# A state scan whose halves are exchanged on VectorE, and queries formed already turned, in a fused S5 + MLA + MoE layer

## The reference, cut to what matters

```python
bu_r = jnp.einsum('lbgp,gnp->lbgn', ul, bbr)
bu_i = jnp.einsum('lbgp,gnp->lbgn', ul, bbi)
_, _, h_r, h_i = lax.associative_scan(_ssm_combine, (a_r, a_i, bu_r, bu_i), reverse=(d == 1), axis=0)
y = y + einsum('lbgn,gpn->lbgp', h_r, c_re[d]) - einsum('lbgn,gpn->lbgp', h_i, c_im[d])
...
q = (_rms_norm(c_q, q_norm_g) @ w_uq).reshape(bsz, seq, N_HEADS, 64 + 32)
q_rope = _rope(q[..., 64:], cos, sin)          # [t1*cos - t2*sin, t1*sin + t2*cos]
s = (einsum('bqhd,bkhd->bhqk', qn, k_nope) + einsum('bqhr,bkr->bhqk', qr, k_rope)) * scale
p = softmax(s);  o = einsum('bhqk,bkhd->bqhd', p, v)
```

## Time and profile before

| what | value |
|---|---|
| time, median of 3 runs (lowest to highest) | 1645.67 us (1643.55 to 1646.66) |
| the profiled execution: its time, its span | 1644.44 us, 1642.6 us |
| PE, DVE, ACT, POOL busy over the span | 93 %, 49 %, 25 %, 26 % |
| one head (scores of step 0 to scores of step 0 of the next, fourth head) | 326.87 to 383.73 us, 56.86 us |

### The profile page before, as it was taken

The page is one execution under the profiler, slowest core; times in us unless marked ns, Lnnn a source line. Parts: engine busy times, 40 slices in busy tenths (PEclk is TensorE's granted clock), DMA queues, the critical chain, the costliest instruction groups (busy, mean ns, idle before and its releaser), DMA issues. The chain is left out here.

```text
span 1642.6 us, 18705 instructions
## 1 busy us (share of the span) xinstructions
PE 1524.1 (93%) x5878; PEld 857.1 (52%) x5878; DVE 797.0 (49%) x1578; ACT 407.0 (25%) x712; POOL 432.8 (26%) x444
## 2 busy tenths in 40 slices
PE   7996999999999979999989999999999999999980
PEld 4545778777777754555534444444444444444430
DVE  1485766777666742488824333333333333333325
ACT  1313554555555441122100001001101001101105
POOL 0000000000000000023423455555555555555520
PEclk9998999999999989999999999999999999999995
DMA  9005000000021018010546999999999999999956
GB/s 256 20 26 68 14 15 14 10 13 10 10 90 25 16 48 310 40 39 27 219 161 230 368 367 367 375 358 360 376 366 354 370 360 360 368 366 359 338 138 218
DMA packets 107457, 321.51 MB, mean 196 GB/s; under 512 B 39638, under 2 KB 56686, under 8 KB 82450
## 3 DMA queue, kind: packets, MB, share of 16 engines
q1 hardware_dynamic: 84002, 261.47, 42.7%
q0 software_dynamic: 23408, 59.45, 15.0%
HBM read 275.93 MB, written 51.72 MB: 199 GB/s over the span
## 5 line engine op out<-in xcount | busy, mean ns | idle before, releaser
L1777 DVE STREAM_TRANSPOSE moe_xgT<-moe_xg 128x1024 f32<-128x1024 f32 x65 | 132.0, 2031 | 421.3 <-DMA moe_xg<-x_d,moe_idx 421.3
L1592 POOL DMA_INDIRECT moe_xg<-x_d,moe_idx x260 | 263.5, 1013 | 116.1 <-issue 60.6
L1172 POOL DMA_INDIRECT slot_d<-all_entry,all_dest_i x48 | 48.0, 1000 | 770.4 <-DVE all_dest_i L1418 758.2
L1666 PE MATMUL moe_p_y<-mixers_ring_b,moe_hT 128*128 128x512 f32 x520 | 233.9, 592 | 0.9 <-DVE moe_hT L1788 0.9
L1646 PE MATMUL moe_p_gu<-mixers_ring_b,moe_xgT 128*128 128x512 f32 x512 | 225.0, 592 | 0.0
L1714 ACT ACTIVATE moe_sig<-moe_p_gu 128x256 f32<-128x256 f32 x65 | 25.0, 384 | 586.6 <-PE moe_p_gu L1646 586.6
L1603 POOL DMA_INDIRECT sum_d<-moe_y,moe_idx x65 | 105.4, 1622 | 244.8 <-DMA sum_d<-moe_y,moe_idx 208.0
L1666 PEld LDWEIGHTS moe_p_y<-mixers_ring_b,moe_hT 128*128 128x128 f32 x520 | 98.7, 190 | 125.0 <-issue 123.9
L1646 PEld LDWEIGHTS moe_p_gu<-mixers_ring_b,moe_xgT 128*128 128x128 f32 x512 | 95.1, 191 | 107.1 <-issue 107.1
L762 PE MATMUL att_p_o<-att_v,att_prT 128*128 128x64 f32 x1024 | 125.5, 276 | 9.5 <-ACT att_prT L852 9.5
L762 PEld LDWEIGHTS att_p_o<-att_v,att_prT 128*128 128x128 f32 x1024 | 119.3, 192 | 26.0 <-ACT att_prT L852 26.0
(11 more groups left out here) (329 smaller groups left out, 1936.0 us busy)
## 6 DMA issues: line engine op xcount, KB each, us to landing
mixers_ring_b<-in_we_down_dram SPq DMA_DIRECT2D x65, 1024.0 KB, 10.1
mixers_ring_b<-in_we_gate_dram SPq DMA_DIRECT2D x32, 1024.0 KB, 10.3
mixers_ring_b<-in_we_up_dram SPq DMA_DIRECT2D x32, 1024.0 KB, 17.5
mixers_ring_a<-in_we_gate_dram SPq DMA_DIRECT2D x17, 1024.0 KB, 10.0
mixers_ring_a<-in_we_up_dram SPq DMA_DIRECT2D x17, 1024.0 KB, 16.9
mixers_o<-in_we_gate_dram SPq DMA_DIRECT2D x16, 1024.0 KB, 10.1
mixers_o<-in_we_up_dram SPq DMA_DIRECT2D x16, 1024.0 KB, 17.2
all_x_sb<-in_x_dram SPq DMA_DIRECT2D x16, 512.0 KB, 9.6
```

The costliest lines, as they stand in the source:

```text
L1172: nc.gpsimd.indirect_dma_start(k.slot_d[:, :], bass.IndirectOffsetOnAxis(ap=k.dest[:, n:n + 1], axis=0), k.entry[:, t, q, :], None).then_i ...
L1592: nc.gpsimd.indirect_dma_start(xg[:, u, g, :], None, x1_quarters, bass.IndirectOffsetOnAxis(ap=idx[:, c, g:g + 1], axis=0), bounds_check=N ...
L1666: last = nc.tensor.matmul(p_y[:, half * 512:(half + 1) * 512], hT[:, u, kk, :], k.moe_dn[v][:, kk * D + half * 512:kk * D + (half + 1) * 512],
L1777: nc.vector.transpose(xgT[:, u].rearrange("p k (g i) -> p g k i", g=NQ), xg[:, u].rearrange("p g (j k) -> p g k j", k=KD)).then_inc(x_turn ...
```

## The change

Four things change.

1. The scan's halves are now exchanged on DVE. `effects` makes one product per group instead of two (4 instead of 8 in each of its calls), into its own half of `p_v` for each direction. `states` gets the swapped product by two instructions on 64 partitions each, which read one half and write the other (`crossed`), both before and after the scan, and adds the two scaled copies into one `gc`. `outputs` then has 3 products per group instead of 5 (12 instead of 20), and `ed2`, `gsn` and `other_edge` are gone.
2. The queries come out of PE already turned: 2 parts of 2 products with 512 moving columns each take the place of 2 parts of 8 products with 96 columns, and the parts "qT" (2 parts of 4 transposes) are gone. There are 5 parts in a head instead of 7, so "v" moves from step 6 to step 4.
3. The query weights hold the 32 rotary columns twice, the second time with halves swapped, so that the 128 rows of a product hold all that the rotation needs. DVE multiplies the 64 rotary rows by a table of cosines and signed sines (`keep_rope`, one instruction of 64 x 512 per part); `rotate` (6 instructions of 128 x 128) is gone. The keys' rotary rows are stored twice, so the score product contracts over 128 rows instead of 96. ACT copies only the 64 rows without rotation, raises the new semaphore `q_nope`, and DVE raises `part_kept` for the query parts.
4. The loading of a head's weights takes 4 DMAs instead of 2, and one more DMA brings the table.

The core of the diff:

```diff
 def load_heads(eng, k, h, u):
-    eng.dma_start(k.wq[:, u], k.w_uq[0].rearrange("(k p) n -> p k n", p=P)[:, :, bass.ds(h * DQ, DQ)]).then_inc(k.head_in[u], 16)
+    eng.dma_start(k.wq[:, u, :, 0:DQ], wq[:, :, bass.ds(h * DQ, DQ)]).then_inc(k.head_in[u], 16)
+    eng.dma_start(k.wq[:, u, :, DQ:DQ + 16], wq[:, :, bass.ds(h * DQ + (NOPE + 16), 16)]).then_inc(k.head_in[u], 16)
+    eng.dma_start(k.wq[:, u, :, DQ + 16:P], wq[:, :, bass.ds(h * DQ + NOPE, 16)]).then_inc(k.head_in[u], 16)
...
-        PARTS = ("q", "q", "k", "k", "qT", "qT", "v")
+        PARTS = ("q", "q", "k", "k", "v")
...
                 if what == "q":
-                    for r in range(4):
-                        t = second * 4 + r
-                        for kk in range(2):
-                            last = nc.tensor.matmul(p_p[:, r * DQ:(r + 1) * DQ], k.cqT[:, kk, t * P:(t + 1) * P],
-                                                    wq[:, u, kk, :], start=(kk == 0), stop=(kk == 1))
+                    for kk in range(2):
+                        last = nc.tensor.matmul(p_p[:, :], wq[:, u, kk, :], k.cqT[:, kk, second * 512:(second + 1) * 512],
+                                                start=(kk == 0), stop=(kk == 1))
...
             def effects(b, d):
-                for part in range(2):
-                    for r in range(GB):
-                        last = nc.tensor.matmul(p_v[:, part, r, :], vsT[:, d * GB + r, part * N:part * N + P],
-                                                U[:, bass.ds(b * GB + r, 1), :].rearrange("p a n -> p (a n)"), start=True, stop=True)
+                for r in range(GB):
+                    last = nc.tensor.matmul(p_v[:, d, r, :], vsT[:, d * GB + r, :],
+                                            U[:, bass.ds(b * GB + r, 1), :].rearrange("p a n -> p (a n)"), start=True, stop=True)
...
-                        nc.tensor.matmul(out, ed1[:, gd, 1 - d:1 - d + T, :].rearrange("p j c -> p (j c)"), gc[:, gd, d:d + NC],
-                                         start=False, stop=False)
-                        last = nc.tensor.matmul(out, ed2[:, gd].rearrange("p j c -> p (j c)"), gsn[:, gd, d:d + NC],
+                        last = nc.tensor.matmul(out, ed1[:, gd, 1 - d:1 - d + T, :].rearrange("p j c -> p (j c)"), gc[:, gd, d:d + NC],
                                                 start=False, stop=(d == 1))
...
+            def keep_rope(h, u, second, p_p=p_p):
+
+                cols = slice(second * 512, (second + 1) * 512)
+                dve.wait_ge(q_nope, h * 2 + second + 1)
+                nc.vector.scalar_tensor_tensor(qT[NOPE:P, u, cols], p_p[NOPE:P, :], SCALE, k.rope[NOPE:P, cols],
+                                               ALU.mult, ALU.mult).then_inc(part_kept, 1)
...
+            def crossed(ch, src, sin_t):
+
+                nc.vector.tensor_tensor(rb[0:N], src[N:P], sin_t[N:P], ALU.mult)
+                ch.link(nc.vector.tensor_tensor(rb[N:P], src[0:N], sin_t[0:N], ALU.mult))
...
-                tt(ra, p_v[:, 0], cos_t[:, own_rows, :], ALU.mult)
-                ch.link(tt(rb, p_v[:, 1], sin_t[:, own_rows, :], ALU.mult))
+                tt(ra, p_v[:, d], cos_t[:, own_rows, :], ALU.mult)
+                crossed(ch, p_v[:, d], sin_t[:, own_rows, :])
                 dve.sem_inc(v_read, 1)
-                ch.link(tt(ra, ra, rb, ALU.add))
+                ch.link(tt(ra, ra, rb, ALU.subtract))
...
-                tt(gc[:, own_rows, off:off + NC], gr[:, :, :], cos_t[:, own_rows, :], ALU.mult)
-                tt(gsn[:, own_rows, off:off + NC], gr[:, :, :], sin_t[:, own_rows, :], ALU.mult).then_inc(g_done, 1)
+                tt(ra, gr[:, :, :], cos_t[:, own_rows, :], ALU.mult)
+                crossed(ch, gr, sin_t[:, own_rows, :])
+                tt(gc[:, own_rows, off:off + NC], ra, rb, ALU.add).then_inc(g_done, 1)
...
                     if t == 0:
                         states(chs, h, u, 0)
                     if t == 1:
                         add_kernels(h)
-                        other_edge(chs, h, 0)
                     if t == 2:
                         states(chs, h, u, 1)
-                    if following and t == ROTATE:
-                        rotate(ch, h + 1)
+                    if following and t < 2:
+                        keep_rope(h + 1, 1 - u, t)
```

More of the change, by code:

```diff
@@ L668, in part @@
                                             start=True, stop=True)
-                elif what == "v":
+                else:
                     for t in range(T):
@@ L672, in part @@
                                                 start=True, stop=True)
-                else:
-                    if second == 0:
-                        pe.wait_ge(q_rotated, h + 1)
-                    for r in range(4):
-                        last = nc.tensor.transpose(p_p[0:DQ, r * P:(r + 1) * P], q[:, second * 4 + r, :], k.ident)
                 last.then_inc(part_done, 1)
@@ L770, in head @@
                         kernels(h, 0)
-                    if following and t in (5, 6):
-                        pe.wait_ge(part_kept, kept + t + 1)
-                        turn_vs(h + 1, t - 5)
+                    if following and t == 5:
+                        pe.wait_ge(part_kept, kept + NP)
+                        turn_vs(h + 1, 0)
+                    if following and t == 6:
+                        pe.wait_ge(vsT_kept, h * 2 + 3)
+                        turn_vs(h + 1, 1)
                     if following and t == 7:
@@ L776, in head @@
                         kernels(h + 1, 1)
[L778 removed]
+            pe.wait_ge(w_in[0], 64)
             pe.wait_ge(k.u_read, 8)
@@ L805, in keep_part @@
                 act.wait_ge(part_done, h * NP + (i + 1) if nth is None else nth)
+                cols = slice(second * 512, (second + 1) * 512)
                 if what == "q":
-                    last = nc.scalar.activation(q[:, 4 * second:4 * second + 4, :].rearrange("p t n -> p (t n)"), p_p[:, 0:4 * DQ], ACT.Copy)
+                    nc.scalar.activation(qT[0:NOPE, u, cols], p_p[0:NOPE, :], ACT.Copy, scale=SCALE).then_inc(q_nope, 1)
                 elif what == "k":
-                    last = nc.scalar.activation(kT[0:NOPE, u, second * 512:(second + 1) * 512], p_p[0:NOPE, :], ACT.Copy)
-                elif what == "v":
-                    last = nc.scalar.activation(v[:, u].rearrange("p t n -> p (t n)"), p_p[:, :], ACT.Copy)
-                else:
-                    last = nc.scalar.activation(qT[:, u, second * 512:(second + 1) * 512], p_p[0:DQ, :], ACT.Copy, scale=SCALE)
-                last.then_inc(part_kept, 1)
+                    nc.scalar.activation(kT[0:NOPE, u, cols], p_p[0:NOPE, :], ACT.Copy).then_inc(part_kept, 1)
+                else:
+                    nc.scalar.activation(v[:, u].rearrange("p t n -> p (t n)"), p_p[:, :], ACT.Copy).then_inc(part_kept, 1)
             def exponent(n, t):
@@ L998, in head @@
                         inputs(chs, h + 1, t - 4)
-                    if following and t == 5:
-                        other_edge(chs, h + 1, 1)
                     if following and t in (6, 7):
@@ L1014, in _ @@
             dve.wait_ge(k.u_read, 8)
-            for g in (gc, gsn):
-                nc.vector.memset(g[:, 0:GB, 0:1], 0.0)
-                nc.vector.memset(g[:, GB:NG, NC:NC + 1], 0.0)
+            dve.wait_ge(k.cT_read, T)
+            nc.vector.memset(gc[:, 0:GB, 0:1], 0.0)
+            nc.vector.memset(gc[:, GB:NG, NC:NC + 1], 0.0)
             dve.sem_inc(o_read, 1)
@@ L1022, in _ @@
             inputs(chs, 0, 0)
+            dve.wait_ge(k.rope_in, 16)
+            keep_rope(0, 0, 0, banks[0])
             inputs(chs, 0, 1)
-            rotate(Chain(dve, own), 0, 3)
+            keep_rope(0, 0, 1, banks[0])
             edge(chs, 0, 1)
@@ L1027, in _ @@
             edge(chs, 0, 0)
-            other_edge(chs, 0, 1)
             assert chs.n == FIRST
```

80 lines of the change are left out of this document (32 added, 48 removed).

## The result

The changed kernel takes 1698.83 us (median of 4 runs, 1697.55 to 1700.13), the one before, run beside it, 1645.35 us (4 runs, 1643.55 to 1646.66). The ratio is 1.0334, with an interval of 1.0322 to 1.0346: 3.3 % slower. The profiled execution took 1698.47 us, its span 1696.7 us, at a mean granted clock of 0.956 (0.977 before).

The account below looks back on a forecast made before the run. PE, busy 93 % of the span, was taken to bound the kernel. The profiled 1644.44 us plus 27.7 us at full clock, mainly a new wait for DVE, and 20 us of lowered clock gave 1692 us, range 1665 to 1708.

Parts of the forecast that it names:

- more than forecast: Rival: both waits lower the clock in nearly every head, or crossed instructions cost 0.83 and more; from 1705 us, chance 0.12.
- DVE's part: DVE's `states`, three more instructions a call: from 4.94 to 7.31 us, +2.37.
- the rival that lived on it: Rival: half-width DVE instructions take half of 0.7 us, `states` 1.4 us shorter than forecast; 1660 us, chance 0.05.
- The new wait in step 0: A head's first step: PE's `kernels` waits for `keep_rope` behind `states(h, 0)` on DVE; +5.06 us in each of 7 heads.
- Step 3: A head's fourth step: `outputs` ready 2.37 us later, then 1.82 us shorter; +0.55, its wait growing from 0.64 to 3.0 us.
- PE's savings: Fewer PE products per head: -0.90 and -0.83 us in the two `effects` calls, -1.82 in `outputs` if its data is there.
- Step 7: A head's last step: `effects` takes half of its 1.81 us, the remainder mostly PE-bound; -0.83 us.
- Steps 4 to 6: Late steps of a head: dropping the "qT" transposes gives 0, moving "v" costs a little; 17.82 us before, +0.2.
- The last head and the tail: Last head: later `states` calls and 12 instead of 20 products, partly at low clock; about +1 us.
- Sum at full clock: One head +4.08 us, seven heads +28.6; with the stage's start and last head, +27.7 us in total.
- The clock: Falls to half speed behind PE's waits: seven at 2.35 us, 16.5, plus one or two more, 3.5; +20 us, bounds 0 and 33.
- Faster: Rival: DVE's extra work hidden, PE's savings alone, -3.35 us a head; 1619 us, chance 0.04.

Follow-up runs that it names:

- experiment 2: Changed kernel plus unused PE transposes of the identity in its two waits (40 ahead of `kernels`, 24 ahead of `outputs`); 1673.73 us, ratio 1.0173.
- experiment 11: Changed kernel with ACT copying all query rows, `outputs` and ACT's sine tables a step later, and `states(h, 1)` cut over two steps; 1612.63 us, ratio 0.9818.
- experiment 10: Kernel before the change, with only `outputs` and ACT's sine tables moved a step later; 1630.91 us, ratio 0.9921.
- experiment 5: Changed kernel with DVE's `keep_rope` moved between the crossed products and the scans of `states(h, 0)`; 1651.39 us, ratio 1.005.
- experiment 1: Changed kernel, but ACT copies all 128 query rows and frees `p_p`, DVE multiplies the rotary rows later in SBUF; 1645.46 us, ratio 1.0004.
- experiment 3: Kernel before the change with only the scan's half of it (new `effects`, `states`, `outputs`), queries as before; 1647.17 us, ratio 1.0018.
- experiment 4: Kernel before the change with only the query and key half of it, `states` as before, table loaded a stage later; 1675.36 us, ratio 1.0183.
- experiment 7: Changed kernel with ACT copying all query rows and `outputs` moved behind the v product of the same step; 1647.46 us, ratio 1.0018.
- experiment 8: Kernel before the change with only `outputs` moved behind the v product of the same step; 1666.59 us, ratio 1.0161.
- experiment 6: Changed kernel with only `outputs` moved behind the v product of the same step; 1673.99 us, ratio 1.0191.

## Why the prediction was right

The sign, the places and the size of the two waits were right, and the predicted 1692 us lies 7 us under the median, inside its range. One term of the sum was mis-sized, the clock's: it came out as the rival "more than forecast" had it, at a chance of 0.12, and that the time still stayed near the forecast was in part luck. By the prediction's own steps:

- **DVE's part.** `states` was put at 7.31 us. It takes 351.62 to 358.89, 7.27. The crossed instructions start 0.69 and 0.71 us after their predecessors of 0.68 and 0.69 us; 0.71 was taken, of 0.60 to 0.83. The trace agrees with the rule that was weighed here (the Trainium skill, "VectorE: DVE Perf Modes", section "Two Vector instructions with no wait between them"). Half the partitions saved nothing, as the row of 64 partitions said; the rival that lived on it is out.
- **The new wait in step 0.** Forecast 5.06 us, with PE starting 11.37 us into the head; it starts 359.68 - 348.46 = 11.22 into it, with 4.91 us idle. Right, 7 times, as forecast.
- **Step 3.** The wait at `outputs` was to grow from 0.64 to 3.0 us and is 2.98. At a held clock the step takes 11.53 us (scores at 361.68 and 373.21 in experiment 2); 350.37 - 347.75 + 8.35 = 10.97 before, that is +0.56 for the forecast +0.55.
- **PE's savings.** Step 7 went from 7.19 to 6.40 us, -0.79 for -0.83. Steps 4 to 6 take 18.02 us instead of 17.82, the +0.2 forecast. The first `effects` takes 2.08 us instead of 3.78 and the stage starts 1.4 us earlier, for 1.9. A wait that the prediction did not have, 2.96 us of the second query part for `keep_rope` ahead of the first head, cost nothing, since the wait for U behind it shrank from 11.72 to 8.27 us. The last head and the tail give +0.9, for +1; the wait for the DMAs of `att_kt` there grew from 7.61 to 9.97 us, so PE's shorter `outputs` won nothing.
- **Sum at full clock.** One head +4.08 forecast, 60.8 - 56.87 = +3.9 measured in experiment 2. Its seven heads take 430.5 us, 426.7 without the idle time of 2.54 us and the fall behind it (1.3), 398.1 before: 28.6 us for 28.6.
- **The clock: the term that was off.** Forecast +20 us, measured 64.67 - 60.8 = 3.9 us in the fourth head, and 452.7 - 426.7 = 26 us over the seven. The fall at the step 0 wait was rightly priced: steps 0 and 1 take 13.03 + 8.47 us, 12.20 + 7.04 with the clock held, 2.26 us lost for the 2.35 taken. The count was wrong: "The 3.0 us wait in step 3 may bring it too; I count one or two more of them in all, 3.5." It brings it in every head: step 3 takes 13.16 us, 11.53 with the clock held, 1.63 us lost, times 7 is 11.4. So there are 14 falls, the seven of step 3 at 11.4 us together and the seven of step 0 at the rest of the 26, 14.6. The rival "more than forecast" had exactly this condition, and priced each fall at 2.35; the smaller price of the second, which was not foreseen, kept the time under its 1705. The pattern of a loop that falls to the low clock in each round, from the Trainium skill ("TensorE: Matmul & The Clock Gate", section "HAM oscillation — how this bites in real kernels"), is what the windows show, twice a head here.
- **The rival on the other side.** "Faster" was worked out as PE's savings standing alone, 3.35 us a head and 1619 us, if DVE's work were hidden. The savings exist: with the clock at 1.00 in both, heads take 52.9 us in experiment 11 and 56.1 in experiment 10, 3.2 us less. The prediction was right that the change as written does not get them, and said that `keep_rope` ahead of `states` would be the way out; experiment 5 shows that this removes the wait in step 0 but leaves the one in step 3. It took the early release of `p_p` (ACT's copy), `outputs` a step later and the cut of `states(h, 1)` together.

What stays open is what decides whether the clock falls behind a short wait. In experiments 1 and 3 one head in seven keeps its clock over a wait of 3.0 us, in experiment 4 one over 2.6; the head of experiment 1 that keeps it takes 11.54 us in step 3 and the others 13.0 to 13.2, which is the price of 1.6 us once more, within one kernel.

## What to carry to other kernels

When a signal moves from one engine to another, read what stands ahead of it in the new engine's order: here a copy of 0.7 us became a wait of 4.9 because it stood behind 7.3 us of other work, and giving the signal back to ACT was worth 53 us. An instruction that looks movable because it waits may itself be cover for another engine (`outputs` hid 5 us of ACT's tables), so run the control that moves it in the old kernel. A long chain on a shared engine can be cut where its consumer is a step away: ACT's copy, the later `outputs` and the cut of `states(h, 1)` together turned a 3.3 % loss into a 1.8 % gain, of which 0.8 % came from the place of `outputs` and would have been had without the change.

## What the runs showed of the hardware that was not expected

- Behind idle times of PE of 2 to 3 us the granted clock fell often, but not always, and the length alone does not decide it. Behind 2.9 to 3.0 us at `outputs` it fell in all seven heads of the changed kernel and of experiment 5, and in six of seven in experiments 1 and 3; behind 2.13 us in six of seven in experiments 7 and 8, and in two of seven in experiment 6. The forecast had counted on such a fall once or twice in seven. One such wait cost nothing at the clock, 1.6 us or 3.3 us (experiment 8, step 3: 12.34, 13.97 and 15.60 us).
- Matmuls that nobody uses are worth their place in a stall: 64 transposes of the identity a head kept the clock at 1.00 behind both waits and made the kernel 25 us faster than without them. Removing the stalls, with `outputs` a step later, was worth far more (86 us).
